# GpSimd takes four weight low parts and both output gate passes of the recurrence, and the first projection is cut into 392 and 256 columns

## The reference

```python
h = x @ w_in
c_q, k, v, k_idx, w_idx = jnp.split(
    h, [Q_LORA_RANK, Q_LORA_RANK + ATT_KV_DIM, Q_LORA_RANK + 2 * ATT_KV_DIM,
        Q_LORA_RANK + 2 * ATT_KV_DIM + IDX_DIM], axis=-1)
...
def hgrn2_mixer(x, lb, w_in, g_norm, w_o):
    h = x @ w_in
    q, f, i, g = jnp.split(h, [HGRN_F_DIM, 2 * HGRN_F_DIM, 2 * HGRN_F_DIM + D_MODEL], axis=-1)
    q = jax.nn.silu(q.astype(jnp.float32))
    fg = lb + (1.0 - lb) * jax.nn.sigmoid(f.astype(jnp.float32))
    k = 1.0 - fg
    logf = jnp.log(fg)
    ...
    o = chunk_gated_linear(heads(q, HGRN_EXPAND), heads(k, HGRN_EXPAND),
                           heads(i.astype(jnp.float32), HGRN_V_DIM), heads(logf, HGRN_EXPAND))
    o = jnp.transpose(o, (0, 2, 1, 3))
    o = rms_norm(o, g_norm) * jax.nn.silu(g.astype(jnp.float32).reshape(B, T, HGRN_HEADS, HGRN_V_DIM))
    return o.reshape(B, T, D_MODEL).astype(dt) @ w_o
```

## Time and profile before

| | |
|---|---|
| median of 3 runs | 949.01 us (948.93 to 949.58) |
| profiled execution, its own time | 951.03 us |
| its span, first to last instruction | 949.0 us |
| busy: PE, PEld, DVE, ACT, POOL | 97%, 80%, 62%, 48%, 16% |
| mean granted TensorE clock | 0.994 |

### The profile page before, as it was taken

The page is one execution under the profiler, slowest core; times in us unless marked ns, Lnnn a source line. Parts: engine busy times, 40 slices in busy tenths (PEclk is TensorE's granted clock), DMA queues, the critical chain, the costliest instruction groups (busy, mean ns, idle before and its releaser), DMA issues.

```text
span 949.0 us, 13816 instructions
## 1 busy us (share of the span) xinstructions
PE 923.1 (97%) x5667; PEld 760.8 (80%) x5667; DVE 590.3 (62%) x957; ACT 457.8 (48%) x609; POOL 156.0 (16%) x128
## 2 busy tenths in 40 slices
PE   8989999999999999899999999999999999999996
PEld 6867788888887997688888888878777788888885
DVE  5874774554648579978736456494223567777775
ACT  5775352433433443543425343345656465564653
POOL 3283300000005500013000000040355201010011
PEclk9999999999999999999999999999999999999999
DMA  8981466555646644245755555449432465555531
GB/s 292 208 163 46 148 228 198 179 179 192 204 143 217 221 147 166 92 131 178 245 178 179 192 199 185 164 158 320 133 134 89 155 207 185 185 178 178 180 130 45
DMA packets 104382, 164.98 MB, mean 174 GB/s; under 512 B 4011, under 2 KB 74714, under 8 KB 104320
## 3 DMA queue, kind: packets, MB, share of 16 engines
q1 hardware_dynamic: 101056, 152.61, 48.6%
q0 software_dynamic: 3264, 11.49, 5.6%
HBM read 159.89 MB, written 4.19 MB: 173 GB/s over the span
## 4 chain that ended last, share of the span: by engine, by line
PE 84%; DVE 8%; ACT 4%; DMA 1%; issue 1%; POOL 1%; SPq 0%; DVEq 0%; POOLq 0%; ACTq 0%
PE PG L1791 12%; PE PA L1791 12%; PE PG L1793 12%; PE PG L1792 12%; PE PA L1793 12%; PE PA L1792 11%; DVE wlo L600 1%; DVE work L1516 1%; ACT whi L591 1%; PE PG L1927 1%; PE TB L2379 1%; PE TB L2042 1%; PE TB L1947 1%; PE PA L2196 1%; PE PA L2195 1%
## 5 line engine op out<-in xcount | busy, mean ns | idle before, releaser
L600 DVE TENSOR_TENSOR wlo<-raw,whi 128x2048 fp32r<-128x2048 f32 (+1 forms) x124 | 288.9, 2346 | 65.5 <-ACT whi L591 65.4
L591 ACT ACTIVATE whi<-raw 128x2048 fp32r<-128x2048 f32 (+1 forms) x142 | 268.7, 1908 | 49.9 <-PE PA L1793 18.7
L1791 PE MATMUL PG<-whi,xlo 128*128 128x512 f32 x548 | 218.4, 399 | 0.3 <-DVE xlo L1098 0.2
L1793 PE MATMUL PG<-whi,xhi 128*128 128x512 f32 x548 | 214.1, 391 | 0.0
L1792 PE MATMUL PG<-wlo,xhi 128*128 128x512 f32 x548 | 213.9, 390 | 0.0
L1793 PEld LDWEIGHTS PG<-whi,xhi 128*128 128x128 f32 x548 | 103.1, 188 | 22.0
L1791 PEld LDWEIGHTS PG<-whi,xlo 128*128 128x128 f32 x548 | 103.2, 188 | 21.8 <-DVE wlo L1322 0.8
L1792 PEld LDWEIGHTS PG<-wlo,xhi 128*128 128x128 f32 x548 | 103.3, 189 | 20.1
L1791 PE MATMUL PA<-whi,xlo 128*128 128x512 f32 (+1 forms) x292 | 117.1, 401 | 1.8 <-DVE xlo L1098 1.3
L1793 PE MATMUL PA<-whi,xhi 128*128 128x512 f32 (+1 forms) x292 | 112.5, 385 | 0.0
L1792 PE MATMUL PA<-wlo,xhi 128*128 128x512 f32 (+1 forms) x292 | 112.2, 384 | 0.0
(11 more groups left out here) (289 smaller groups left out, 1175.3 us busy)
## 6 DMA issues: line engine op xcount, KB each, us to landing
raw<-in_ffn_w_gate SPq DMA_DIRECT2D x44, 512.0 KB, 4.0
raw<-in_ffn_w_up SPq DMA_DIRECT2D x44, 512.0 KB, 5.0
raw<-in_ffn_w_down SPq DMA_DIRECT2D x22, 1024.0 KB, 4.8
raw<-in_w_up SPq DMA_DIRECT2D x44, 512.0 KB, 4.6
raw<-in_hgrn_w_in SPq DMA_DIRECT2D x16, 1024.0 KB, 5.3
raw<-in_w_qkv SPq DMA_DIRECT2D x12, 1024.0 KB, 5.3
raw<-in_w_down SPq DMA_DIRECT2D x11, 1024.0 KB, 4.8
raw<-in_att_w_o SPq DMA_DIRECT2D x4, 1024.0 KB, 5.8
```

The lines of the kernel that those rows point to most:

```text
L591: nc.scalar.activation(whi[:, g, 0:n_], raw[:, s, 0:n_], ACT.Copy).then_inc(S("w_hi"), 1)
L600: nc.vector.tensor_tensor(wlo[:, s, 0:n_], raw[:, s, 0:n_], whi[:, g, 0:n_].bitcast(F32), ALU.subtract).then_inc(S("w_lo"), 1)
L1791: mm(dst, xl[:, k, rows], whi[:, g, cols], start=first, stop=False)
L1793: return mm(dst, xh[:, k, rows], whi[:, g, cols], start=False, stop=last_)
```

## The change

1. The low parts of `U_H + 13` to `U_H + 16` move from VectorE, where they stood between the levels, to GpSimd.
2. The two output gate passes move from VectorE to GpSimd, behind those low parts; `gated` waits for them (`g_made`).
3. The first projection is cut anew: units 0 and 1 hold the columns 0 to 255 and 512 to 647, 392 in all, and unit 2 the 256 between them. With that ScalarE's and VectorE's work there is reordered: the low part of unit 2 is made after the angles, that of unit 3 after the norm, the high part of unit 3, the sine and the high part of unit 4 later.
4. The high parts of `U_AO + 2` and `U_AO + 3` are made after pairs 2 and 4 instead of 0 and 1.

```diff
-SKIP, EARLY = 392, 256
-C_V, C_KI, C_WI, C_K = 248, 376, 504, 512
+EARLY, SKIP = 256, 512
+FIRST = EARLY + IN_COLS - SKIP
+C_KI, C_WI, C_K, C_V = 256, 384, 392, 520
...
             pool.memset(aT[:, 0:2, :, :], 0.0).then_inc(S("hconst"), 1)
+            for u in range(U_H + 13, U_H + 17):
+                lo_unit(u)
+            pool.wait_ge(S("g_sig"), 1)
+            link(pool.tensor_tensor(flat(sg), flat(sg), flat(fT), ALU.mult))
+            pool.wait_ge(S("gno"), 16)
+            gv = flat(sg).rearrange("p (g c) -> p g c", c=DH)
+            pool.tensor_tensor(gv, gv, gno.unsqueeze(1).broadcast_to([P, RT * HH, DH]), ALU.mult)\
+                .then_inc(S("g_made"), 1)
...
             hi(2)
-            hi(3)
-
-            act.wait_ge(S("ang"), 1)
-            ac.activation(trig.rearrange("p a b c -> p (a b c)"), ang.rearrange("p a b c -> p (a b c)"),
-                          ACT.Sin).then_inc(S("trig"), 1)
             full(1)
-            ac.activation(pin[:, :, 0:512], PG[:, :, :], ACT.Copy).then_inc(S("pin"), 1)
+            ac.activation(pin[:, :, 0:FIRST], PG[:, :, 0:FIRST], ACT.Copy).then_inc(S("pin"), 1)
...
-            hi(4)
+            hi(3)
+            act.wait_ge(S("ang"), 1)
+            ac.activation(trig.rearrange("p a b c -> p (a b c)"), ang.rearrange("p a b c -> p (a b c)"),
+                          ACT.Sin).then_inc(S("trig"), 1)
             turned(ev["cq"])
             ac.activation(flat(xhi[:, 0:2, :]), TB[:, ev["cq"] % 2, :], ACT.Copy).then_inc(S("x_hi"), 1)
-            act.wait_ge(S("cqn"), 1)
+            hi(4)
...
-                if p < 2:
-                    hi(U_AO + 2 + p)
+                if p in (2, 4):
+                    hi(U_AO + 1 + p // 2)
...
             x_lo_rows("x", 1)
-            lo(2)
...
-            lo(3)
-
+            lo(2)
             vec.wait_ge(S("pin"), 1)
...
             ins.then_inc(S("cqn"), 1)
+            lo(3)
+            lo_of_bank(flat(xlo[:, 0:2, :]), ev["cq"], flat(xhi[:, 0:2, :]))
...
             take(MASKED)
-            lo(U_H + 13)
             decayed(0)
             take(0)
-            lo(U_H + 14)
             decayed(1)
             take(1)
-            lo(U_H + 15)
             decayed(2)
             take(2)
-            lo(U_H + 16)
             decayed(3)
             take(3)
             decayed(4)
-            vec.wait_ge(S("g_sig"), 1)
-            link(ve_.tensor_tensor(flat(sg), flat(sg), flat(fT), ALU.mult))
             decayed(5)
-            vec.wait_ge(S("gno"), 16)
-            gv = flat(sg).rearrange("p (g c) -> p g c", c=DH)
-            link(ve_.tensor_tensor(gv, gv, gno.unsqueeze(1).broadcast_to([P, RT * HH, DH]), ALU.mult))
...
+            vec.wait_ge(S("w_lo"), U_H + 17)
             lo(U_H + 17)
...
             def gated(b, bank):
+                vec.wait_ge(S("g_made"), 1)
```

More of the change, by code:

```diff
@@ L90, in weight_units @@
     v = w_in.rearrange("(t p) n -> p t n", p=P)
-    a = [[v[:, 4 * j:4 * j + 4, c:c + EARLY] for c in (0, SKIP)] for j in range(2)]
+    a = [[(0, v[:, 4 * j:4 * j + 4, 0:EARLY]), (EARLY, v[:, 4 * j:4 * j + 4, SKIP:IN_COLS])] for j in range(2)]
     a.append([(0, 8, SKIP - EARLY, v[:, :, EARLY:SKIP])])
@@ L407, in _ @@
                 for g, landed_ in enumerate((f"first_loaded{u}", f"w_loaded{u}")):
-                    dst = raw[:, u, g * UNIT // 2:(g + 1) * UNIT // 2].rearrange("p (t s c) -> p t s c", s=2, c=EARLY)
-                    for s, view in enumerate(units[u]):
-                        sp.dma_start(dst[:, :, s, :], view[:, 2 * g:2 * g + 2, :]).then_inc(S(landed_), 16)
+                    dst = raw[:, u, g * 2 * FIRST:(g + 1) * 2 * FIRST].rearrange("p (t c) -> p t c", t=2)
+                    for o, view in units[u]:
+                        sp.dma_start(dst[:, :, o:o + view.shape[2]], view[:, 2 * g:2 * g + 2, :]).then_inc(S(landed_), 16)
             sp.dma_start(h[:, 1, :], hv[:, 1, :]).then_inc(S("x_loaded1"), 16)
@@ L578, in unit_len @@
         def unit_len(u):
[L579 removed]
+            return 4 * FIRST if u < 2 else UNIT
         def hi(u):
@@ L758, in _ @@
             x_hi_rows("x", 0)
-            first, second = slice(0, UNIT // 2), slice(UNIT // 2, UNIT)
+            first, second = slice(0, 2 * FIRST), slice(2 * FIRST, 4 * FIRST)
             for u in range(2):
@@ L766, in _ @@
             hi(2)
+            full(1)
+            ac.activation(pin[:, :, 0:FIRST], PG[:, :, 0:FIRST], ACT.Copy).then_inc(S("pin"), 1)
+            act.wait_ge(S("pin"), 1)
+            for r in range(RT):
+                ac.activation(sq[:, r, :], pin[:, r, 0:NQL], ACT.Square,
+                              accum_out=ve[:, 8 + r:9 + r]).then_inc(S("ssq"), 1)
             hi(3)
@@ L771, in _ @@
                           ACT.Sin).then_inc(S("trig"), 1)
-            full(1)
-            ac.activation(pin[:, :, 0:512], PG[:, :, :], ACT.Copy).then_inc(S("pin"), 1)
-            act.wait_ge(S("pin"), 1)
-            for r in range(RT):
-                ac.activation(sq[:, r, :], pin[:, r, 0:NQL], ACT.Square,
-                              accum_out=ve[:, 8 + r:9 + r]).then_inc(S("ssq"), 1)
-            hi(4)
             turned(ev["cq"])
             ac.activation(flat(xhi[:, 0:2, :]), TB[:, ev["cq"] % 2, :], ACT.Copy).then_inc(S("x_hi"), 1)
-            act.wait_ge(S("cqn"), 1)
+            hi(4)
             full(2)
             ac.activation(pin[:, :, C_K:C_K + P], PA[:, 2:4, 0:P], ACT.Copy).then_inc(S("k_in"), 1)
-            ac.activation(pin[:, :, C_V:EARLY], PA[:, 2:4, P:SKIP - EARLY], ACT.Copy).then_inc(S("k_in"), 1)
+            ac.activation(pin[:, :, C_V:C_V + P], PA[:, 2:4, P:SKIP - EARLY], ACT.Copy).then_inc(S("k_in"), 1)
             hi(5)
@@ L1318, in _ @@
             for u in range(2):
-                for part, made, done in ((slice(0, UNIT // 2), "first_hi", "first_lo"),
-                                         (slice(UNIT // 2, UNIT), "w_hi", "w_lo")):
+                for part, made, done in ((slice(0, 2 * FIRST), "first_hi", "first_lo"),
+                                         (slice(2 * FIRST, 4 * FIRST), "w_hi", "w_lo")):
                     vec.wait_ge(S(made), u + 1)
@@ L1816, in turn_and_up @@
                                 parts_ready(ev[name] + 2 * r + k // 4)
-                            last = products(bank(r), k, r, u + s, slice(t * 512, (t + 1) * 512), k == 0, k == KT - 1)
+                            n_ = 512 if u else FIRST
+                            last = products(bank(r)[:, 0:n_], k, r, u + s, slice(t * n_, (t + 1) * n_), k == 0, k == KT - 1)
                         if r == RT - 1:
@@ L2077, in later_columns @@
                     for r in range(RT):
-                        last = products(PA[:, 2 + r, 0:136], k, r, U_IN + 2, slice(k * 136, (k + 1) * 136), k == 0,
+                        last = products(PA[:, 2 + r, 0:256], k, r, U_IN + 2, slice(k * 256, (k + 1) * 256), k == 0,
                                         k == KT - 1)
```

1 line of the change is left out of this document (removed).

## The result

The changed kernel takes 960.98 us (median of 4 runs, 959.9 to 962.61) against 949.3 us before (4 runs on the same chip, 948.93 to 949.81). The ratio is 1.0119 with a 95% interval of [1.0105, 1.0133]: slower by 1.2%, 11.7 us. 957.5 was forecast, with a range of 942 to 963. The profiled execution took 959.9 us of its own time, with a span of 958.0.

The account below looks back on a forecast made before the run. TensorE, busy 97%, was taken to bound most of the kernel, VectorE's chain the recurrence up to 401.5 us. 949.0 + 9.0 (recurrence) + 1.5 (clock) - 1.4 (in-projection) - 0.6 (high parts) = 957.5 us, range 942 to 963.

Parts of the forecast that it names:

- full hold: Recurrence: each 4.6 us GpSimd pass blocks VectorE's two-SBUF-input operations throughout; 957.5 us, chance 0.50 with GpSimd in the gaps.
- The bound: Whole kernel: TensorE busy 97%; among long stretches only the recurrence, up to 401.5 us, pays for time off VectorE.
- The count without holds: Recurrence: if VectorE's 12.9 us come off unhindered, level 4 at 385.3, cross term at 396.1, 5.1 us earlier.
- Four low parts 4, gate passes 5: Recurrence: the moved low parts alone make the cross term 4 us late, the gate passes bring another 5.
- The clock, 1.5: Recurrence: longer waits add one stretch of TensorE at the 1.2 GHz level, 1.5 us, bounds none and 4.5.
- The in-projection, 1.4: First projection: products of 392 and 256 columns and an earlier unit 2 gain 1.4 us, bounds 0 and 2.4.
- The later high parts, 0.6: First attention: two high parts moved behind pairs 2 and 4 gain net 0.6 us, bounds 0 and 1.4.
- The sum: Whole kernel: 949.0 + 9.0 + 1.5 - 1.4 - 0.6 = 957.5 us span, and the median the same.
- GpSimd in the gaps: Recurrence: a waiting GpSimd pass gets in between two adjoining VectorE operations; with holds of full length 957.5 us, chance 0.50.
- VectorE goes first: Recurrence rival: adjoining decay products keep GpSimd out, low parts cost nothing, cross term 4 us late; 951 us, chance 0.15.
- No hold, 942: Recurrence rival: long GpSimd passes let VectorE through at decay products of levels 0 to 5; 942 us, chance 0.20.
- It costs more, 963: Recurrence rival: masked copies are held too, 16 us late, 963 us; or clock losses of 4.5 us, 961; chance 0.15.

Follow-up runs that it names:

- tiny: The changed kernel with GpSimd's six recurrence passes over 16 columns instead of 2,048, TensorE reading high parts for those low parts; 947.00 us, ratio 0.9965.
- writes: The changed kernel with GpSimd's six passes replaced by memsets of the same places, nearly as long, TensorE reading high parts for low parts; 945.83 us, ratio 0.9957.
- one_input: The changed kernel with each of GpSimd's six passes replaced by two one-input copies, TensorE reading high parts for low parts; 957.71 us, ratio 1.0085.
- gates_back: The changed kernel with the two gate passes back on VectorE, the four low parts staying on GpSimd; 953.22 us, ratio 1.0034.
- front_only: The kernel before with only the new in-projection cut and the two later high parts, the recurrence as it was; 948.93 us, ratio 0.9990.
- late_hi: The kernel before with the two later high parts alone; 949.51 us, ratio 0.9996.
- gates_only: front_only with the two gate passes alone on GpSimd, the low parts staying on VectorE; 957.78 us, ratio 1.0082.

## Why the prediction was right, step by step

The direction, the mechanism and most of the size came as forecast. The median stands 3.5 us above the likeliest value of 957.5, just inside the 954.5 to 961 that the full hold was given. That the span came so much nearer (957.5 forecast, 958.0 measured) is partly luck, told below under the sum.

**The bound.** Right. The chain did run on VectorE in the recurrence and hardly elsewhere. The limit was nearer than I had it: 12.9 us taken off VectorE give 3.0 (tiny) to 3.3 us (writes). The count without holds put the cross term at 396.1, which is 5.4 us early (the 5.1 written there is a slip, of 0.3 us in the 942), a distance of 37.4; tiny has 39.8. Of these 2.4 us 1.0 lies ahead of level 4 (27.6 us from the diagonal in tiny, 26.6 in the count), where TensorE itself has hardly a gap (0.68 us at level 2), and 1.4 behind it (12.2 against 10.8), where ScalarE's copies behind its sigmoid bind.

**The full hold.** Right, with nothing beyond the pass's own length: products of 0.68 us became 3.6 to 5.1 us long, that is held by 2.9 to 4.4, each hold ending with GpSimd's pass. The step by step count gives for levels 1, 2, 3, 4 and 5, in the kernel before's time, 373.1, 380.5, 387.0, 393.8 and 404.6. The trace, with 2.16 us added for the earlier diagonal, has 373.10, 380.93, 387.11, 394.23 and 404.56. That GpSimd's pass excludes a VectorE product with two SBUF inputs for the whole instruction is what the Trainium skill states in "SBUF — State Buffer", section "SBUF: two separate sides". The same section of the Trainium skill adds that this is so only against a GpSimd operation that reads SBUF, and writes (945.83 us, products of 0.68) and one_input (957.71 us, products of 2.2 to 2.4) agree with it on both sides. With that clause of the Trainium skill alone, one_input could have been forecast; I had left it aside.

**Four low parts 4, gate passes 5.** The low parts are 4.3 (gates_back against front_only) to 4.4. The gate passes are 5.5 between levels 4 and 5; the count had them right there. Behind level 5 it gave 5.8 us to the cross term. At the full clock level 5 to level 6 takes 2.7 us (gates_back) and level 6 to the cross term 3.5 (the changed kernel, with no gate pass on VectorE there), together 6.2: 0.4 us too little.

**The clock, 1.5.** One stretch was forecast beyond the one before, two came (372.4 to 375.8 and 399.7 to 406.5). The second cost 2.0 us ahead of level 6 (4.7 against 2.7 us from level 5). The first used up time in which level 2 would have waited for VectorE anyway, and cost at most 0.4 us (level 2 at 380.93 against 380.5). Recurrence and clock together: 10.5 forecast, 11.2 measured by distance; level 5 itself was 9.9 us late in both.

**The in-projection, 1.4.** The mis-sized term: the spacings came as forecast (0.178 and 0.120 against 0.177 and 0.120), but TensorE waited 1.05 us for the last small load, which I had taken to be in time.

**The later high parts, 0.6.** Wrong, zero: late_hi measures 0.9996 [0.9988, 1.0005]. The 0.3 to 0.5 us late twice were seen, and what I took as gain at pairs 1 and 2 was wholly given back. Together these two terms were 2.0 and measured 0.55 (front_only).

**The sum.** 9.0 + 1.5 - 2.0 = 8.5 us was forecast, 11.7 measured. 1.45 of the 3.2 us are the front and 0.7 the recurrence. The remaining 1.1 us is as much as the median (960.98) stands above the profiled execution (959.9), in which the distances were taken. The two profiled executions differ by 8.9 us, which is 11.2 less the 2.16 that the changed kernel's is ahead at the diagonal; but only about 0.55 of these are the change's doing. The windows of the kernel before and of the changed kernel show most of the rest, a stretch at the lower clock in the first attention that only the execution of before has. In late_hi, whose recurrence and first projection are those of before, this stretch is at the full clock (1.00), and the diagonal begins at 357.41, 1.3 us earlier than in before:

```profile
53.60:57.10 3.50, 3.50 (x15) 2.36 (x13) 3.10 (x16) 0.00 (x0) 1.83 (x2) 0.51 1.01 173
```

```profile
53.60:57.10 3.50, 3.50 (x25) 2.77 (x25) 2.52 (x14) 1.82 (x6) 2.02 (x1) 1.00 1.01 170
```

The prediction set the profiled execution's own time against the median and found 2.0 us, and took the same distance for the new kernel; part of it was this stretch. In the changed kernel the profiled execution lies 1.1 us below the median and not 2.0 above it. So the span's near hit rests on two errors that cancel: 2.0 us were forecast for the two parts at the front, which gave 0.55, and the stretch in the execution of before made up for the rest.

**GpSimd in the gaps.** Right for the changed kernel (363.87, 5.08 us; 397.37, 4.98 us: GpSimd's next pass got in between two adjoining products), but no rule: in gates_only four adjoining products kept GpSimd out for 2.4 us. The rival "VectorE goes first" thus exists, but it made nothing cheap there: the pass came later and held the products of level 5 instead of those of level 4, for 7.9 us of distance.

**No hold, 942.** Excluded, and its price was too good: 947.0 and 945.8 measured.

**It costs more, 963.** Its reason, that masked copies are held too, is excluded: they kept 2.47 and 2.19 us with a pass under way.

## What to carry to other kernels

In this kernel GpSimd's reading passes and VectorE's products with two SBUF inputs are one queue: moving such work from one to the other costs GpSimd's length (4.6 us) in the place of VectorE's (2.1), on VectorE's own path. It was free under VectorE's copies from PSUM, so cut the pass to that window (2.4 us under 2.5 us of copies) and release it by the semaphore that opens the window. And before giving a bound engine relief, look at who binds next: here 1.9 us of sigmoid in ScalarE's queue ahead of the copies that the next level waited for; a change of order took 1.0 us off the stretch behind level 4.

## What the runs showed of the hardware that I had not expected

- A GpSimd copy with one SBUF input (1.90 us alone) excludes VectorE's two-input products as a two-input pass does: products of 2.17 to 2.38 us. Memsets of the same places don't.
- Who goes next is not one rule. GpSimd got in after the first of adjoining products in the change and in one_input, and was kept out for all four (6.91 us for a 4.55 us pass) in gates_only, whose second pass then did get in behind the first product of level 5 (397.61, 4.97 us). What tells these apart wasn't tried and stays open.
- Where they alternate, both pay: GpSimd's piece of 512 columns goes from 1.28 to 1.6 or 1.75 us, VectorE's product from 0.68 to 1.77.
